# Hybrid decoder step on Trainium2: the first pair of each stage as eight plain products, the first tokens normalised by halves, and all of x loaded ahead of the first weights

## The reference, cut to what matters

```
a = rmsnorm(x, g_mix);  u = a @ w_in            # q, k, v, gates, o, and conv channels B, C, h
h = mLSTM(q, k, v, gates) * sigmoid(o);  y = B * conv3(C * h_c)
x += concat(h, y) @ w_out
f = rmsnorm(x, g_ffn);  x += (silu(f @ w_gate) * (f @ w_up)) @ w_down     # width 2816
e = rmsnorm(p @ w_ple, g_ple);  x += sigmoid(x @ w_pg) * e
y = rmsnorm(x, g_final)
```

## Time and profile before

| what | before |
|---|---|
| median of 3 runs | 2670.49 us (2669.78 to 2672.49) |
| the profiled execution | 2669.71 us |
| its span in the trace | 2668.0 us |
| PE busy | 2504.5 us, 94% |
| DVE, ACT, POOL busy | 55%, 34%, 39% |
| mean granted TensorE clock | 0.976 |

### The profile page before, as it was taken

The page is one execution under the profiler, slowest core; times in us unless marked ns, Lnnn a source line. Parts: engine busy times, 40 slices in busy tenths (PEclk is TensorE's granted clock), DMA queues, the critical chain, the costliest instruction groups (busy, mean ns, idle before and its releaser), DMA issues.

```text
span 2668.0 us, 41317 instructions
## 1 busy us (share of the span) xinstructions
PE 2504.5 (94%) x15882; PEld 2441.3 (92%) x15882; DVE 1477.2 (55%) x2291; ACT 906.4 (34%) x1691; POOL 1043.4 (39%) x863
## 2 busy tenths in 40 slices
PE   4899798999999989999999999998999999999997
PEld 3899687999999989999999999998899999999997
DVE  4666787765565574466643333477347664333355
ACT  4335353433333533333421112343234432212233
POOL 3566655666676332322331222323322323222233
PEclk6999898999999999999999999999999999999998
DMA  5555644666576656566456455575557555554544
GB/s 166 194 185 189 229 167 166 221 223 227 206 252 231 209 157 212 167 228 197 158 182 206 149 169 171 175 220 186 183 177 234 181 199 167 197 193 163 174 144 158
DMA packets 292392, 507.86 MB, mean 190 GB/s; under 512 B 23892, under 2 KB 188037, under 8 KB 291687
## 3 DMA queue, kind: packets, MB, share of 16 engines
q1 hardware_dynamic: 211846, 272.28, 30.3%
q10 hardware_dynamic: 80352, 232.94, 26.8%
HBM read 378.89 MB, written 126.27 MB: 189 GB/s over the span
## 4 chain that ended last, share of the span: by engine, by line
PE 68%; DVE 9%; DMA 5%; issue 3%; POOL 2%; ACT 1%; DVEq 0%; POOLq 0%; SPq 0%; ACTq 0%
PE bank L547 22%; PE bank L549 21%; PE bank L548 21%; DMA wring<-weight_parts 3%; POOL wring L2498 2%; DMA weight_parts<-wring 1%; DVE qlo L1645 1%; PE bank L647 1%; DVE sg L2357 1%; DVE ess L2229 1%; PE bank L658 1%; DMA wraw<-w_gate 0%; PE bank L710 0%; DMA xs<-x_prompt 0%; PE bank L637 0%
## 5 line engine op out<-in xcount | busy, mean ns | idle before, releaser
L547 PE MATMUL bank<-qhi,wring 128*128 128x352 f32 (+1 forms) x3588 | 1176.9, 328 | 104.6 <-issue 20.1
L2498 POOL TENSOR_TENSOR wring<-wraw,wring 128x512 fp32r<-128x512 f32 x528 | 769.7, 1467 | 1278.5 <-ACT wring L1179 1275.9
L549 PE MATMUL bank<-qhi,wring 128*128 128x352 f32 (+1 forms) x3588 | 1159.1, 323 | 0.0
L548 PE MATMUL bank<-qlo,wring 128*128 128x352 f32 (+1 forms) x3588 | 1158.0, 323 | 0.0
L547 PEld LDWEIGHTS bank<-qhi,wring 128*128 128x128 f32 x3588 | 685.9, 191 | 132.8 <-issue 115.2
L548 PEld LDWEIGHTS bank<-qlo,wring 128*128 128x128 f32 x3588 | 685.7, 191 | 0.0
L549 PEld LDWEIGHTS bank<-qhi,wring 128*128 128x128 f32 x3588 | 683.6, 191 | 0.0
L1179 ACT ACTIVATE wring<-wraw 128x512 fp32r<-128x512 f32 x528 | 329.4, 628 | 755.0 <-PE bank L549 593.9
L547 PE MATMUL bank<-hid,wring 128*128 128x352 f32 (+1 forms) x1056 | 340.7, 323 | 11.8 <-DVE wide L2316 7.1
L549 PE MATMUL bank<-hid,wring 128*128 128x352 f32 (+1 forms) x1056 | 339.2, 321 | 0.0
L548 PE MATMUL bank<-hid,wring 128*128 128x352 f32 (+1 forms) x1056 | 338.2, 320 | 0.0
(11 more groups left out here) (305 smaller groups left out, 2441.7 us busy)
## 6 DMA issues: line engine op xcount, KB each, us to landing
wring<-weight_parts ACTq DMA_DIRECT2D x428, 512.0 KB, 4.5
weight_parts<-wring SPq DMA_DIRECT2D x206, 512.0 KB, 3.8
wraw<-w_down SPq DMA_DIRECT2D x33, 1024.0 KB, 7.1
wraw<-w_in SPq DMA_DIRECT2D x12, 1024.0 KB, 6.9
wraw<-w_in SPq DMA_DIRECT2D x48, 256.0 KB, 4.4
wraw<-w_gate SPq DMA_DIRECT2D x11, 1024.0 KB, 6.5
wraw<-w_up SPq DMA_DIRECT2D x11, 1024.0 KB, 6.2
wraw<-w_gate SPq DMA_DIRECT2D x44, 256.0 KB, 3.5
```

The costliest lines, as they stand in the source:

```text
L547: nc.tensor.matmul(o, hi, mh, start=begins, stop=False, skip_group_check=True)
L548: nc.tensor.matmul(o, hi, ml, start=False, stop=False, skip_group_check=True)
L549: return nc.tensor.matmul(o, lo, mh, start=False, stop=ends, skip_group_check=True)
L2498: nc.gpsimd.tensor_tensor(wlo[e % RING][:, :].rearrange(v, k=k), w.src, whi[e % RING][:, :].rearrange(v, k=k), ALU.subtract).then_inc(lo_d ...
```

## The change

- The first pairs of `in`, `out` and gate (`PLAIN_PAIRS`) are computed by eight plain products, 96 matmuls, in the order A11 B11, A21 B11, A12 B21, A22 B21, A11 B12, A21 B12, A12 B22, A22 B22, on four banks. They need no sums of weights and no sums of blocks, but B12 as an operand of its own (`B12`, kept where operand 6 lies). Four ring entries serve eight products, so `ahead()` is called at products 0, 5, 6 and 7 only.
- These pairs' weights are no longer written to DRAM and read back: each super loads 1 MB raw and makes four entries.
- The duos are gone: out 1 and up 0 are ordinary seven-product pairs behind the plain one.
- T1, T2, T4 and T3 are made during or after the plain pair. T3 (operand 6) must wait for the last use of B12, which in `in` is the end of the gates.
- The gates multiply B12 itself, four block products instead of five.
- ACT evicts the plain pairs of `in` and gate, DVE that of `out`.
- Tokens are normalised by halves: roots of tiles 0 to 2 and then 3 to 5, spreads at pg products 11 and 15, B11 and B21 at 12 and 13, B12 and B22 at 17 and 18. In super 0 the result goes to another buffer (`q.A`), so it waits for no store.
- At the start all six x tiles are issued ahead of the first weights; the gains come as rows of 128 in five transfers and are transposed by PE; SP, not ACT, issues super 0's x stores; ACT starts without waiting for POOL's constants.

```
-SOURCES = {"in": (0, 4, 1, 2, 5, 6, 3), "out": (0, 4, 5, 6, 3), ...
+SOURCES = {"in": (0, 1, 7, 2, 4, 5, 3, 6), "out": (0, 7, 4, 5, 3, 6), ...
+B12 = 7
+PLAIN_PAIRS = {("in", 0): (0, 1, 2, 6), ("out", 0): (0, 1, 2, 3), ("gate", 0): (0, 1, 2, 6)}
+PLAIN_ENTRIES = ("A11", "A21", "A12", "A22")
+PLAIN_PRODUCTS = (("a", 0, 0, 0), ("b", 1, 0, 1), ("P2", 2, 1, 0), ("P4", 3, 1, 1),
+                  ("c", 0, B12, 2), ("d", 1, B12, 3), ("P3", 2, 2, 2), ("P5", 3, 2, 3))
+PLAIN_AHEADS = (0, 5, 6, 7)
+X_BANKS = ((0, 1), (2, 3), (4, 5), (2, 3), (4, 5), (6, 2))
...
+        q.A = R if q.n else q.U
...
 # PE
+            def plain_pair(q, st, i, after, base):
+                banks, stage, e = banks_of(st, i), st if st in STAGES else "ffn", n_entry[0]
+                for j, (name, n, op, corner) in enumerate(PLAIN_PRODUCTS):
+                    bk, starts = banks[corner], j in (0, 1, 4, 5)
...
+                    entry_ready(e + n)
+                    operand_ready(q, stage, op)
+                    if starts:
+                        take(bk)
+                    for k in range(4):
+                        last = three(bank[bk][:, 0:q.N], hi[:, k, :], lo[:, k, :], qhi[:, slot(op), k, 0:q.N],
+                                     qlo[:, slot(op), k, 0:q.N], starts and k == 0, not starts and k == 3)
...
-                for b, terms in enumerate((((0, 0), (1, 1)), ((0, 0), (0, 4), (1, 2)))):
+                for b, terms in enumerate((((0, 0), (1, 1)), ((0, B12), (1, 2)))):
...
-                if DUO_OUT:
-                    duo(q, ("out", 0), ("out", 1), out_after(q))
+                plain_pair(q, "out", 0, out_after(q), 0)
...
+                plain_pair(q, "gate", 0, ffn_after(q), 0)
+                pair(q, "up", 0, ffn_after(q), 7)
...
 # SP, start
             for t in range(NTILE):
                 sp.dma_start(xin[t][0:q.tiles[t][1], :], x_source(q, t)).then_inc(xin_in[t], 16)
                 if t == 2:
-                    raw()
-                    sp.dma_start(gmix[:, :], g_mix[0].rearrange("(c p) -> p c", p=P)).then_inc(gmix_in, 16)
+                    gains_rows()
             raw()
+            first_x_stores((0, 1, 2))
             constants()
+            raw()
+            first_x_stores((3, 4, 5))
...
 # ACT
+            def plain_pair(q, st, i, evict, after, base):
+                for j, (name, n, op, corner) in enumerate(PLAIN_PRODUCTS):
+                    if j in PLAIN_AHEADS:
+                        ahead()
+                    if evict is not None and j % 4 > 1:
+                        act.wait_ge(*written[(q.n, st, i, name)])
+                        evict(corner % 2, corner // 2, banks_of(st, i)[corner])
+                    if j < 7:
+                        after(base + j)
...
+            def first_gate_after(q):
+                def after(s):
+                    if s < 4:
+                        high_of(q, "ffn", (2, 4, 5, 3)[s])
...
+            for t in range(3):
+                first_squares(t)
+            act.wait_ge(consts_made, 1)
+            ahead()
+            high_of(q, "in", 0)
+            first_squares(3)
+            x_evict(q, 3, X_BANKS[3][0], 0)
+            ahead()
+            first_squares(4)
+            x_evict(q, 4, X_BANKS[4][0], 0)
+            high_of(q, "in", 1)
+            first_squares(5)
+            x_evict(q, 5, X_BANKS[5][0], 0)
+            ahead()
+            ahead()
+            high_of(q, "in", B12)
+            high_of(q, "in", 2)
...
+                plain_pair(q, "in", 0, in_evict(q), in_after(q), 0)
+                ahead()
+                ahead()
+                high_of(q, "in", 6)
...
 # DVE, pg_after
-                    for at_, part in ((16, "B11"), (17, "T1"), (18, "B21"), (19, "B22"), (20, "T2"), (23, "T3")):
+                    for at_, part in ((12, "B11"), (13, "B21"), (17, "B12"), (18, "B22"), (25, "T1"), (27, "T2")):
...
-                    for i in (6, 3):
-                        low_of(nxt, "in", i)
...
 # POOL, start
+            roots_of_x(supers[0], 0)
+            ahead()
+            ahead()
+            roots_of_x(supers[0], 1)
+            ahead()
+            ahead()
```

More of the change, by code:

```diff
@@ L359, in add_pairs @@
-        if two and not stored:
-            duo_raws.append((made[0][0], made[1][0]))
-    def add_pair(q, st, i, w, c0, spares=None):
-        add_pairs(q, [(st, i)], [(w, c0)], product_order(st, i), spares or {})
+            turn = {n: n_sums[0] + j + 1 for j, n in enumerate(turns)}
+            n_sums[0] += 4
+            shift = [sum(1 for k in spares if k < j) for j in range(len(names))]
+            where = {n: e0 + j + shift[j] for j, n in enumerate(names)}
+            for j, n in zip((0, 1, 3, 6), turns):
+                sums_at.setdefault(e0 + j + shift[j], []).append((n, r, at_, where, turn))
@@ new lines, in add_pair @@
+        for j, n in enumerate(names):
+            if n in views:
+                add_entry(r, views[n], turn.get(n, 0), n == first)
+                if not stored and (n in turn or n == "A11"):
+                    keep_entry(of, n)
+                end[r] = n_prepared[0]
+            else:
+                n_loads[0] += 1
+                entries.append(Entry(r, None, 0, False, None, None, kept_as[(of, n)]))
+                entries[-1].loads = n_loads[0]
+            if j in spares:
+                add_spare(r, spares[j])
@@ L1538, in _ @@
                 high_of(q, "out", 1)
-                if DUO_OUT:
-                    duo(q, ("out", 0), ("out", 1), None, out_after(q))
-                for i in range(2 if DUO_OUT else 0, 4):
+                high_of(q, "out", 2)
+                plain_pair(q, "out", 0, None, out_after(q), 0)
+                for i in range(1, 4):
                     pair(q, "out", i, None, out_after(q), 7 * i)
                 embedding(q)
-                high_of(q, "ffn", 4)
-                if DUO_FFN:
-                    duo(q, ("gate", 0), ("up", 0), sl[:, 0, q.blocks[0]], ffn_first(q), ACT.Silu)
@@ L1547, in _ @@
-                for p in range(1 if DUO_FFN else 0, FFP):
+                high_of(q, "ffn", B12)
+                plain_pair(q, "gate", 0, gate_evict(q), first_gate_after(q), 0)
+                pair(q, "up", 0, None, up_after(q, 0), 0)
+                for p in range(1, FFP):
                     pair(q, "gate", p, sl[:, 0, q.blocks[0]], gate_after(q, p), 0, ACT.Silu)
@@ L2633, in pair, with plain_pair @@
                     after(base + j)
+            def plain_pair(after):
+                for j in range(8):
+                    if j in PLAIN_AHEADS:
+                        ahead()
+                    if j < 7:
+                        after(j)
             def nothing(s):
@@ L2639, in after @@
                 def after(j):
[L2640 removed]
+                    if j == 0:
                         low_of(q, st)
```

755 lines of the change are left out of this document (337 added, 418 removed).

## The result

The changed kernel takes **2686.05 us** (median of 4 runs, 2682.99 to 2692.24) against 2670.14 for the kernel before (4 runs beside it): ratio 1.0061, 95% interval 1.0043 to 1.008. It is slower by 16 us. The prediction was 2612 us, range 2594 to 2640, with 0.95 on faster: wrong in sign and by 74 us.

A forecast was written before the change was run, and what follows sets the result against it. PE, busy 2504.5 of 2668.0 us, was taken to bound the kernel. Terms -25.6 + 3 - 17.7 + 3 - 12 + 8 - 16.7 = -58.0 took 2669.7 to 2612 us, range 2594 to 2640.

The forecast's parts named there:

- Pair after the gates: `in` 1 in each super: T3 only at the gates' end, bank 6 eviction; about 1 us each, +3 (0 to +9).
- Start: Start to the gates' end: 81.6 becomes 56.0 us, -25.6 (bounds 51 and 64), first product near 20.
- `out` and `ffn` of super 0: Fewer DVE sums: `in` 11 to `out` 1 65.7 to 48.0 us (-17.7); PLE to gate 2 117.9 to 106 (-12).
- `ffn` of supers 1 and 2: New wait: weight of up 0's second product asked for late, behind ACT's operand splits; +4 each, +8 (-2 to +12).
- Seams: `pg` to `in`, twice: B11 and B21 normed earlier, low parts after the seam; 43.0 and 41.0 us, -16.7.
- Rival 4: Slower: weights behind operands in ACT's queue in plain pairs, ring dry in 9 first pairs; 2705 us; chance 0.03.
- Rival 1: DVE and POOL serialise, lengthening first pairs' operand chains by 1.1 us in four steps; about 2636 us; chance 0.15.
- Rival 2: Start waits for the first weights, 3.75 MB landing at 24 instead of 16 us; 2620 us; chance 0.12.
- signs that the prediction named as its own refutation: First product later than 28 us; DVE full at seams with PE waiting; POOL's low parts as releaser all over plain pairs.
- the rest: All stages outside the named terms: predicted change 0.

The follow-up runs named there:

- y first: Changed kernel, with VectorE normalising the previous third's first tile of y right after T3, ahead of operand 6's low part and the gates' bias: 2678.6 us.
- the last kernel: Kernel with all edits of order and operand 2 on DVE, plus in `ffn` operand 5 before the first Silu eviction and operand 3 behind operand 6: 2626.3 us.

## Why the prediction was wrong, point by point

**Pair after the gates: +3, measured +33.5. This is the step that failed.** It named T3's chain and found operand 6 in time, which it was. It looked only at operands and at ACT's eviction. It left out what else the diff moves there. The tiles of y went from after products 6 and 10 to after 7 and 11: the first from ahead of T3's chain to behind it, the second from ahead of the DVE step that waits for ACT's chain to behind it. That step moved too, the other way: it stood after product 11 in the kernel before and stands after product 10 now. The pair's order became the five-bank one (P1, P5, P2, P6, P7, P4, P3 in place of P1, P7, P5, P6, P2, P4, P3), so that P5 and P7 are added behind that step too, and P4 wants bank 7, which the forget gate's rows hold until it. The runs bear this out: `in` 1 took 81.1 us in the three supers, 71.8 with y first and 65.6 with the gate's step two products later. With the order mended the pair takes 14.8, 17.9 and 17.5 us against 14.9, 16.7 and 16.1 before: the term of +3 is what the change costs if its queues are right.

**Start: -25.6, measured -17.7.** First product near 20: measured 19.87, right (17.8 to 19.5 in the other runs that don't change the order of x). The miss is behind it. The prediction said that ACT "splits T1, T2 and T4 ahead of the second gate weight" and let the gates run from 48. Operand 3, which is T4, was counted on ACT, but not what waits for it on POOL: the clearing stands after product 4 as before, but the `ahead()` calls that were ahead of it now come behind it. The gates began at 54.8. In the last kernel they begin at 49.0, but still wait 2.8 us there for ACT's eviction.

**`out` and `ffn` of super 0: -17.7 and -12, measured -6.3 and -1.3.** I took DVE's work as reduced by the sums that the plain pairs don't need. Its busy time in the two stages is down by only 0.5 and 5.2 us: the parts that went are short (0.5 to 0.7 us), the low part that came is 1.6, and beside POOL's operand 2 (4.61 us) a single weight sum of `out` 1 took 3.71 us in place of 0.7. I have not split it further. The last kernel has 3 and 6 us of it back: in `out` 2.4 of the 3 came with operand 2 on DVE, in `ffn` 2.6 came with it and 3.7 with the order in `ffn`. The rest stays (DVE 52.8 of 59.4 us busy).

**`ffn` of supers 1 and 2: +8, measured +7.1, right in size.** But the cause was only partly the late weight load: in super 1 PE waited 1.00 us for the load of the weight, 1.87 for POOL's operand 2 and 0.53 for a DVE addition. The order of ACT and DVE in `ffn` brought it to +1.9 with the loads where they were.

**Seams: -16.7, measured -1.2.** PE no longer waits for low parts at the start of `in` 0 but for evictions of `sg` (3.57 us at 944.91), which stand on DVE behind the low part of B12 and T1; then the gate weight. About two thirds of the term were to be had: -10.8 in the last kernel, of which -8.8 came with the weights ahead of operand 3.

**Rivals.** Rival 4, slower by weights behind operands in ACT's queue, had the place right and 14 us of the effect, but its price was of a dry ring in nine pairs; the wait was one weight, at the gates and at `up` 0. Rival 1 (DVE and POOL serialise) is real in single rows, but what it costs in sum was not shown: moving operand 2 changes the load of both engines as well. The argument against it was misread: in the stages of supers 1 and 2 outside `pg` POOL is busy for 26 to 34% of the time, not for a quarter at most. Rival 2, weights at the start, did not decide. None of them held the main loss. Of the signs that the prediction named as its own refutation two came in part: PE waits at the seams, though DVE is less full there than before (32.7 of 50.3 us against 39.7 of 52.0); and POOL's low parts of weights are the first releaser of all, but mostly at the gates and in `out` 1 and `up` 0, behind the plain pairs, while in these PE waited for operand 2 (3.3, 2.6 and 1.9 us the longest).

**Where the gain went.** The change with its queues mended and operand 2 on DVE runs in 2626 us against 2666, 40 us less. How much of that is due to the plain pairs and half norms was not separated: one edit, operand 2 on DVE, could be made in the kernel before as well; that was not tried, nor which of the other edits of order would help it. The change as made lost more than it gained in queues: one instruction that waits, with others behind it whose data was ready.

The +4.0 in the rest need no cause of their own: in the traces of the changed kernel and its variants the rest is between 2004.6 and 2015.2 us. What stays open is `in` 2 of super 0, where PE waits 6.8 us for DVE (5.7 in the kernel before). Ahead of the awaited additions DVE does the two scans (4.7 us) and then the steps of the gates' weights (5.9 us); no run moved either past an addition.

## What to carry to other kernels

When a change alters the order or the banks of a product list, go through each in-order engine's queue across the next pair, also instructions that the diff does not show: for each that waits, write down what is ready behind it and who wants it. Freeing the one resource that the profile names can bring nothing (bank 7) when the releaser is an instruction that itself waits; move that instruction. And price a pause of PE with the clock that follows it, not with its own length.

## What the runs showed of the hardware

**The clock after a pause.** In `in` 1 of super 1 after, by shorter windows:

```profile
974.29:984.00 9.71, 6.84 (x37) 4.89 (x36) 6.53 (x9) 2.25 (x3) 1.83 (x1) 0.93 0.73 214
984.00:990.00 6.00, 6.00 (x22) 5.41 (x21) 0.00 (x0) 1.45 (x4) 0.00 (x0) 0.54 0.36 94
990.00:997.00 7.00, 2.88 (x18) 2.59 (x17) 1.36 (x3) 5.90 (x9) 0.94 (x3) 0.96 0.25 79
997.00:1004.83 7.83, 7.58 (x32) 7.54 (x33) 3.50 (x7) 1.38 (x4) 0.37 (x2) 0.60 0.74 265
```

After the pause of 2.9 us at 981 PE ran without a gap but at a mean granted clock of 0.54, near the lower of its two levels (1.2 of 2.4 GHz), 22 instructions in 6 us where the earlier trace rows has 38 in 6 us; after the 4.4 us at 997 again 0.60. The pauses at 981 and 997 are 7.2 us together, and the pair is 13.9 us longer than before.

**DVE beside POOL.** In the start of the kernel after, DVE and then POOL:

```profile
35.17 1.62 DVE L1841 TENSOR_TENSOR wide<-wide 128x1408 f32<-128x1408 f32 x1
36.83 2.60 DVE L1844 TENSOR_TENSOR mixq<-wide 128x1408 f32<-128x1408 f32 x1
39.36 4.58 DVE L1686 TENSOR_TENSOR qlo<-wide,qhi 128x1408 fp32r<-128x1408 f32 x1
43.87 1.61 DVE L1686 TENSOR_TENSOR qlo<-mixq,qhi 128x1408 fp32r<-128x1408 f32 x1
```

```profile
35.38 2.58 POOL L2508 TENSOR_TENSOR wring<-wraw,wring 128x512 fp32r<-128x512 f32 x1 [5.04 <-ACT wring L1209]
37.92 4.54 POOL L2522 TENSOR_TENSOR qlo<-wide,qhi 128x1408 fp32r<-128x1408 f32 x1
```

POOL's first ends at 37.96 and DVE's 2.60 us instruction 1.47 later; POOL's second ends at 42.46 and DVE's 4.58 us one 1.48 later. Each time DVE's end is POOL's end and about its own length (1.61 us at 43.87), as if it had begun only then. POOL waits in its turn: its second instruction ends 3.03 us after DVE's 2.60 us one, and where the kernel before splits operand 2 on POOL the same instruction takes 3.1 to 3.9 us, not 4.54. The row of 2.71 us at 396.55 in the earlier trace rows is of this kind too: POOL's low part of a weight ends at 397.78, and DVE 1.48 later. The prediction priced such a step at 1.1 us more; the second here costs 3.0.

The Trainium skill, page "SBUF — State Buffer", section "Who interferes with whom", has this as a rule: a DVE instruction with two SBUF inputs contends with a GpSimd instruction that reads SBUF, and the shared ports are an exclusive lock; the page's section "Terms" adds that the lock is held for the full instruction. These rows agree. What all such steps cost together no run shows.
